# Three wide networks in a two-block kernel: the inner tile computed already turned, and its split made in two halves

## What is computed

```python
D_MODEL = 1024
SEQ = 256
D_FF_2 = 4 * D_MODEL
def sq_relu_mlp(h, w1, w2):
    return jnp.square(jax.nn.relu(h @ w1)) @ w2
...
        h_lat = h_lat + g2[:, None, :] * sq_relu_mlp(m_l, mlp_w1[i], mlp_w2[i])
        if ctx_out:
            m_c = modulate(rms_norm(h_ctx, norm_g[i, 1]), csh2, csc2)
            h_ctx = h_ctx + cg2[:, None, :] * sq_relu_mlp(m_c, mlp_w1[i], mlp_w2[i])
```

## Time and profile before

| | us |
|---|---|
| median of 3 executions (2055.31 to 2056.4) | 2055.65 |
| profiled execution | 2055.59 |
| its span | 2053.3 |

### The profile page before, as it was taken

One profiled execution on the slowest core, in us unless ns is written; L12 is line 12 of the kernel. 1 busy time (PEld: TensorE's weight loads), 2 busy tenths in 40 slices (PEclk: granted clock), 3 DMA queues, 4 the chain that ended last, 5 costly groups with the idle time before them and its releaser, 6 DMA issues.

```text
span 2053.3 us, 23941 instructions
## 1 busy us (share of the span) xinstructions
PE 1940.8 (95%) x9559; PEld 1574.3 (77%) x9559; DVE 1151.9 (56%) x1379; ACT 962.0 (47%) x1405; POOL 105.0 (5%) x178
## 2 busy tenths in 40 slices
PE   7999975799999999999999999899989999989997
PEld 5778864677777777787877787788878877877886
DVE  4545665454557445674655656666555456655554
ACT  5444533254446434544554435644454447545442
POOL 2400000000001000000010000000200000100000
PEclk9999986799999999999999999999999999999999
DMA  9867540277656676564476765444545544334551
GB/s 289 259 232 256 179 142 0 73 261 245 227 197 226 233 238 223 186 210 144 167 258 207 234 220 191 153 164 170 188 138 179 190 164 160 107 100 138 203 178 68
DMA packets 234094, 379.68 MB, mean 185 GB/s; under 512 B 12040, under 2 KB 152720, under 8 KB 233984
## 3 DMA queue, kind: packets, MB, share of 16 engines
q1 hardware_dynamic: 231200, 369.69, 52.8%
q0 software_dynamic: 2448, 8.33, 1.6%
q10 hardware_dynamic: 336, 0.14, 0.0%
HBM read 377.06 MB, written 1.05 MB: 184 GB/s over the span
## 4 chain that ended last, share of the span: by engine, by line
PE 88%; DVE 5%; ACT 3%; issue 2%; DMA 1%; POOL 1%; SPq 0%; POOLq 0%; ACTq 0%; DVEq 0%
PE ps L448 26%; PE ps L450 25%; PE ps L449 25%; PE ps L458 5%; PE ps L596 2%; DVE w_lo L1912 1%; ACT w_hi L1317 1%; PE ps L647 1%; PE ps L629 1%; PE ps L1192 1%; PE ps L1171 1%; ACT arena L1442 0%; DVE xt_lo L1937 0%; DMA raw<-ffn_w_in_dram 0%; ACT arena L1344 0%
## 5 line engine op out<-in xcount | busy, mean ns | idle before, releaser
L1912 DVE TENSOR_TENSOR w_lo<-raw,w_hi 128x1024 fp32r<-128x1024 f32 x602 | 718.0, 1225 | 249.7 <-ACT w_hi L1317 247.0
L1317 ACT ACTIVATE w_hi<-raw 128x1024 fp32r<-128x1024 f32 x602 | 613.3, 1056 | 276.5 <-PE ps L450 247.7
L448 PE MATMUL ps<-w_hi,xt_hi 128*128 128x512 f32 x1632 | 649.7, 398 | 18.6 <-DVE xt_lo L2071 11.8
L450 PE MATMUL ps<-w_hi,xt_lo 128*128 128x512 f32 x1632 | 638.4, 391 | 0.0
L449 PE MATMUL ps<-w_lo,xt_hi 128*128 128x512 f32 x1632 | 638.2, 391 | 0.0
L448 PEld LDWEIGHTS ps<-w_hi,xt_hi 128*128 128x128 f32 x1632 | 309.7, 190 | 83.0 <-issue 18.7
L450 PEld LDWEIGHTS ps<-w_hi,xt_lo 128*128 128x128 f32 x1632 | 309.0, 189 | 65.0
L449 PEld LDWEIGHTS ps<-w_lo,xt_hi 128*128 128x128 f32 x1632 | 309.6, 190 | 61.2 <-issue 1.0
L448 PE MATMUL ps<-w_hi,ht_hi 128*128 128x512 f32 x768 | 309.4, 403 | 2.4 <-DVE ht_lo L2455 2.4
L449 PE MATMUL ps<-w_lo,ht_hi 128*128 128x512 f32 x768 | 301.6, 393 | 0.0
L450 PE MATMUL ps<-w_hi,ht_lo 128*128 128x512 f32 x768 | 301.4, 392 | 0.0
(11 more groups left out here) (268 smaller groups left out, 1120.5 us busy)
## 6 DMA issues: line engine op xcount, KB each, us to landing
raw<-mlp_w_dram SPq DMA_DIRECT2D x192, 512.0 KB, 4.3
raw<-ffn_w_in_dram SPq DMA_DIRECT2D x176, 512.0 KB, 5.7
arena<-ada_w_dram SPq DMA_DIRECT2D x96, 512.0 KB, 6.5
raw<-ffn_w_out_dram SPq DMA_DIRECT2D x88, 512.0 KB, 4.5
raw<-odd_w_in_dram SPq DMA_DIRECT2D x48, 512.0 KB, 4.6
raw<-attn_w_qkv_dram SPq DMA_DIRECT2D x24, 512.0 KB, 5.0
raw<-even_w_in_dram SPq DMA_DIRECT2D x22, 512.0 KB, 4.7
raw<-ple_w_gate_dram SPq DMA_DIRECT2D x16, 512.0 KB, 4.3
```

Of the source, the lines that this page charges most:

```text
L448: pe.matmul(dst, a_hi, hi, start=start, stop=False)
L450: return pe.matmul(dst, a_lo, hi, start=False, stop=stop)
L1317: act.activation(w_hi[:, slot, c], raw[:, slot, c], ACT.Copy).then_inc(S(f"hi{slot}"), 1)
L1912: TT(w_lo[:, slot, c], raw[:, slot, c], w_hi[:, slot, c].bitcast(F32), ALU.subtract).then_inc(S(f"lo{slot}"), 1)
```

## The change

The up products inside the loop, seven in each network, become `up_turned`: the weights' columns stand, 128 at a time, and the input of all 256 tokens moves. That gives the inner tile with its columns already on partitions, in banks 4 and 5, each bank holding two groups of 128 columns. A tile takes 8 x 4 x 3 = 96 matmuls with 256 moving columns in place of 48 with 512. `hidden` remains for the first tile of each network alone, since its up product is still the old one. For the other tiles `h1` is already turned, ScalarE and VectorE split it from `h1` in SBUF, and the split has two instructions of 512 elements on each engine in place of one of 1024. TensorE waits for the first half ahead of the first half of the down product and for the second ahead of the second. ScalarE's halves wait until TensorE has read the same half of the tile before out of `ht` (`wait_used(4 - half)`).

```diff
+            def up_turned(j):
+                pe.wait_ge(S("m_h1"), 2 * j + 2)
+                for half in range(2):
+                    slot, uses = ring.take()
+                    for quarter in range(2):
+                        slab(slot, uses, quarter)
+                        for b in range(2):
+                            for t in (2 * quarter, 2 * quarter + 1):
+                                k = 4 * half + t
+                                for i in (2 * b, 2 * b + 1):
+                                    to = ps[:, 4 + b, i % 2 * SEQ:(i % 2 + 1) * SEQ]
+                                    c = t * 512 + i * P
+                                    hi, lo = w_hi[:, slot, c:c + P], w_lo[:, slot, c:c + P]
+                                    pe.matmul(to, hi, xt_hi[:, k, :], start=k == 0 and i % 2 == 0, stop=False,
+                                              skip_group_check=True)
+                                    pe.matmul(to, hi, xt_lo[:, k, :], start=False, stop=False, skip_group_check=True)
+                                    last = pe.matmul(to, lo, xt_hi[:, k, :], start=False, stop=k == KT - 1,
+                                                     skip_group_check=True)
+                            if k == KT - 1 and b == 0:
+                                last.then_inc(S("m_up0"), 1)
+                        last.then_inc(S(f"used{slot}"), 1)
...
             def mlp(job, job_read, last=False):
                 base = MLP_STEPS * n["mlp"]
                 n["mlp"] += 1
+                hidden("m_", base, 4)
                 for i in range(MLP_STEPS - 1):
-                    hidden("m_", base + i, 4)
-                    up(4, "m_up0")
-                    pe.wait_ge(S("m_ht"), base + i + 1)
+                    up_turned(base + i)
                     if i == 0:
                         acc_is_free()
+                        pe.wait_ge(S("m_ht"), 2 * base + 2)
                     job(i)
+                    pe.wait_ge(S("m_ht"), 2 * (base + i) + 1)
                     add_rows(ht_hi, ht_lo, 0, i == 0, False)
+                    pe.wait_ge(S("m_ht"), 2 * (base + i) + 2)
                     add_rows(ht_hi, ht_lo, 2, False, False)
                     job_read(i)
-                hidden("m_", base + MLP_STEPS - 1, 4)
-                pe.wait_ge(S("m_ht"), base + MLP_STEPS)
                 if last:
+                    pe.wait_ge(S("m_ht"), 2 * (base + MLP_STEPS))
                     last_rows(0, ht_hi, ht_lo, fill=False)
                     return
                 job(MLP_STEPS - 1)
+                pe.wait_ge(S("m_ht"), 2 * (base + MLP_STEPS) - 1)
                 add_rows(ht_hi, ht_lo, 0, False, False)
                 job(MLP_STEPS)
+                pe.wait_ge(S("m_ht"), 2 * (base + MLP_STEPS))
                 add_rows(ht_hi, ht_lo, 2, False, True)
...
                 def turned(j):
 
-                    act.wait_ge(S("m_ht_ps"), 2 * j + 2)
-                    act.activation(ht_hi[:], cut(ps[:, 6:8, :].rearrange("p b n -> p (b n)"), 4, SEQ),
-                                   ACT.Copy).then_inc(S("m_ht_hi"), 1)
+                    for half in range(2):
+                        if j == base:
+                            act.wait_ge(S("m_ht_ps"), 2 * j // MLP_STEPS + half + 1)
+                        else:
+                            act.wait_ge(S("m_h1"), 2 * j + half + 1)
+
+                            wait_used(4 - half)
+                        act.activation(ht_hi[:, 2 * half:2 * half + 2, :],
+                                       cut(bank(6 + half) if j == base else h1[:, half, :], 2, SEQ),
+                                       ACT.Copy).then_inc(S("m_ht_hi"), 1)
...
                         dve.wait_ge(S("m_relu"), 2 * j + m + 1)
+                        if j > base:
+
+                            dve.wait_ge(S("m_ht"), 2 * j + m - 1)
                         TT(h1[:, m, :], bank(b0 + m), relu_s[:, m, :], ALU.mult).then_inc(S("m_h1"), 1)
 
                 def ht_low(j):
-                    dve.wait_ge(S("m_ht_hi"), j + 1)
-                    TT(ht_lo[:], cut(ps[:, 6:8, :].rearrange("p b n -> p (b n)"), 4, SEQ), ht_hi[:].bitcast(F32),
-                       ALU.subtract).then_inc(S("m_ht"), 1)
+                    for half in range(2):
+                        dve.wait_ge(S("m_ht_hi"), 2 * j + half + 1)
+                        TT(ht_lo[:, 2 * half:2 * half + 2, :],
+                           cut(bank(6 + half) if j == base else h1[:, half, :], 2, SEQ),
+                           ht_hi[:, 2 * half:2 * half + 2, :].bitcast(F32), ALU.subtract).then_inc(S("m_ht"), 1)
```

## The result

| | before | after |
|---|---|---|
| median, us | 2055.48 (4 runs, 2053.7 to 2056.4) | 2041.28 (4 runs, 2039.19 to 2042.18) |
| profiled execution, us | 2055.59 | 2041.04 |
| its span, us | 2053.3 | 2038.9 |
| mean granted clock | 0.971 | 0.973 |

The ratio is 0.993, with a 95% interval of 0.9913 to 0.9948. The forecast was 2040.9 us, with a range of 2037 to 2047.

What follows compares the result with a forecast made beforehand. TensorE, busy 95% of the span, was taken as the bound. Loops 3.1, first two ends 6.8, third end 1.8 and clock 3.1 us gave 14.8 off 2055.59: 2040.8, as median 2040.9 us, range 2037 to 2047.

Steps and rivals of the forecast that it cites:

- The pitch: Turned up products: matmuls with 256 moving columns start 0.1198 us apart, 0.61 us more a product, 12.9 us over 21.
- The bound below: Up products: no price for the change of weights, 0.107 us a matmul, which would take 26 us off.
- the bound above: Up products: a load not hidden at all, 0.297 us a matmul, 357 us more.
- The turns: Steps two to seven of each network: eight transposes of 0.89 us go 18 times, 16.0 us off.
- list of other edits: Loops: split casts and remainders, new waits and half-wise waiting on TensorE cost nothing under a 10.9 us down product.
- The first two ends: First and second networks' ends: the 3.41 us of turn and wait before the job go, 6.8 us off together.
- The third end: Third network's end: TensorE goes on at 2029.61 in place of 2031.43, 1.8 us off, 1.42 us idle left.
- The clock: Slow matmuls behind the first and third ends' waits go, 1.5 and 1.6 us, 3.1 us off.
- the step that held the waits between networks unchanged: Waits of 3.61 and 3.69 us between networks stay; the sum has no clock gain or loss behind them.
- The rival of the clock: Slow stretches land otherwise behind remaining waits, 1.5 to 1.6 us each, at most 2045.6 us; chance 0.17.
- The second end's DMA: Attention weights' transfer at 1709.44 does not come earlier, so 3.4 us come back: 2044.2 us; chance 0.05.
- The sum: Whole kernel: 3.1 loops, 6.8 first two ends, 1.8 third end, 3.1 clock, 14.8 us off 2055.59.

Runs made afterwards that it cites:

- the width alone: Kernel before, its loop up products cut to 256 moving columns, tokens still standing and turns kept: 2072.73 us, ratio 1.0087.
- the wait ahead of the job: Kernel after, with TensorE waiting for both halves of the eighth tile's split before the job in the first two networks: 2043.68 us.
- a whole split: Kernel after, with one cast and one remainder over 1024 elements per tile in place of halves: 2048.91 us, ratio 0.9969.
- the third end's halves and the second network's first tile: Kernel after, with the third network's last down product waiting half by half and the second network's first up product turned: 2038.15 us, again 2039.01.
- the halves alone: Kernel before, with its split in two halves of 512 elements, up products and all turns kept: 2052.66 us, ratio 0.9987.

## Why the prediction was right

**The pitch** (0.1198 us from another stage's rows, forecast +0.61 us a product): measured 0.1199 and 11.51 us, +0.62. That the input stood in those rows made no difference, as the width alone shows (11.60 us behind transposes, where the turned product has 11.59). The bound below, no price for the load, would be 0.107 us, and the bound above 0.297. Shown.

**The turns** (0.89 us in 18 steps; step of 22.4 us): measured 22.42. The loops gave 2.3 us, not 3.1. Of the difference 0.55 is a wait that the list of other edits had at nothing, 0.31 us of idle time and the restart, for VectorE's `w_lo` ahead of the first network's fourth turned product. Most of the rest is that a changed step took 22.42 us where the sum had 22.66 - 0.89 + 0.61 = 22.38.

**The first two ends** (3.41 us each): no idle time and no turn, as forecast. The runs divide what the prediction took together. With the wait ahead of the job 1.7 us of each come back, with a whole split 1.9.

**The third end** (restart 1.8 us earlier, 1.42 us idle left): 1.50 us idle. Of the difference, 0.08, the cast has 0.03 (0.63 us, not 0.597) and the handings over the rest (0.10 from TensorE to ScalarE, not 0.05). Of the third network's 4.19 us the forecast had 1.0 + 1.8 + 1.6 = 4.4.

**The clock** (-3.1 us: both slow stretches at ends go, nothing else changes): the two went. But the step that held the waits between networks unchanged was off in both directions. Behind the wait into the second network a slow stretch went that was there before, worth 5.72 - 4.4 = 1.3 us; behind the wait for the attention a stretch with four slow matmuls came to hold nine, -1.0 us. They nearly cancel. The rival of the clock named the place and the size (1.5 us a stretch), and did not decide.

**The second end's DMA** held nothing: the gain of the second network, 5.72 us, passed on to the attention's first product.

**The sum**: 14.8 us forecast against the profiled execution, 14.4 in the spans and 14.2 in the medians. That it is right to 0.4 us is partly luck: the loops gave 0.8 us less than forecast, the clock 0.5 more (the two stretches gave 3.3 for 3.1, and the other two 0.3).

What stays open: which waits of between 2.1 and 3.7 us are followed by a slow stretch in a given kernel. It is not chance from one execution to the next, as far as two profiles of each of two kernels show: the kernel after, and the one with the third end's halves and the second network's first tile, had theirs behind the same waits when run again. Small edits move them. A wait of 2.37 us had one at two ends of three before, and at three of three with only the width changed; waits of 3.6 us had none, a short or a long one; the attention's wait of 2.12 us had none in the kernels before and after, and one in others. Nothing here foretells it from the wait's length.

## What to carry to other kernels

A matmul's price in a stream was 0.2268 us at 512 moving columns, 0.1199 at 256 and 0.1114 at 128 with this type, which fits the larger of its moving columns and its load of 128 standing columns. So a product may be turned round at 256 moving columns for 6% of its time (0.62 us of 10.89), if that takes away more work around it, and not at 128. A turn costs little in the middle of a stream (0.89 us), and its worst price is at the end of it, where it stands in a chain of turn, cast and remainder with nothing beside; look there first, and cut what is left in halves so that the first lies beside work that still runs. Where waits can't be removed and slow matmuls stand behind them, matmuls of zeros in the wait are worth a try (5.8 us here, behind three waits; a fourth had nothing to give).

## What the runs showed of the hardware that was not expected

- A stream of fp32r matmuls with 128 moving columns, begun at the granted clock 0.50 behind a wait, stayed at 1.2 GHz for the 41 us of its length with TensorE busy 40.00 of 40 us. The same stream begun at 2.4 GHz kept it. With 256 columns the slow stretches behind waits were over within the first product (11.59 us behind transposes at the full clock, 12.14 to 13.27 behind waits of 3 to 6 us).
- From the first network on, the waits of 1.41 to 1.69 us in these traces had no slow matmuls behind them; among those of 2.12 us and more some had.
- With matmuls of zeros in bf16 the clock stayed at 1.00 over four waits, with 0.56 to 0.81 us of idle time left in each; three of the four had slow matmuls behind them without the zeros.
- Which waits have a slow stretch behind them changes from kernel to kernel, and was the same in two profiles of each of two kernels. Two kernels that differ in one edit can so differ by 1 to 3 us that the edit itself did not cost, as the halves alone show: 3.2 us given at the ends, 2.8 taken elsewhere.
